# A split layer norm, an input taken by tiles, a set-up moved into the first layer and smaller attention-stage products in a two-layer transformer kernel

## What is computed

```python
def layer_norm(x, g, b):
    mu = x.mean(-1, keepdims=True)
    var = jnp.square(x - mu).mean(-1, keepdims=True)
    return (x - mu) * lax.rsqrt(var + LN_EPS) * g + b

h = layer_norm(x, emb_ln_g, emb_ln_b)
for i in range(DEPTH):                       # 2
    mix = hybrid_mixer(h, ...)               # h @ w_in, fox attention, hgrn2, @ w_out
    h = layer_norm(ALPHA * h + mix, ln1_g[i], ln1_b[i])
    ffn = peer_ffn(h, ...)                   # queries, keys, top 16, experts u and v
    ple = sigmoid(h @ ple_gate_w[i]) * (p[i] @ ple_w[i])
    h = layer_norm(ALPHA * h + ffn + ple, ln2_g[i], ln2_b[i])

# fox attention: scores q k^T * scale + c_q - c_k (c: running sum of the forget gate's log)
# hgrn2: A[t, s] = sum_k q[t,k] k[s,k] exp(b[t,k] - b[s,k]) for s <= t, with b a running sum
```

## Time and profile before

| | us |
|---|---|
| median of the runs | 3343.91 (3341.01 to 3344.86, 3 runs) |
| profiled execution | 3346.2 |
| its span, first to last instruction | 3344.4 |
| TensorE busy | 3246.8 (97%) |
| VectorE busy | 2526.8 (76%) |
| GpSimd busy | 2059.4 (62%) |
| ScalarE busy | 1388.8 (42%) |

### The profile page before, as it was taken

The page is one execution under the profiler, slowest core; times in us unless marked ns, Lnnn a source line. Parts: engine busy times, 40 slices in busy tenths (PEclk is TensorE's granted clock), DMA queues, the critical chain, the costliest instruction groups (busy, mean ns, idle before and its releaser), DMA issues. The chain is left out here.

```text
span 3344.4 us, 47104 instructions
## 1 busy us (share of the span) xinstructions
PE 3246.8 (97%) x17370; PEld 2895.4 (87%) x17370; DVE 2526.8 (76%) x4660; ACT 1388.8 (42%) x2738; POOL 2059.4 (62%) x1388
## 2 busy tenths in 40 slices
PE   5999999999999999999999999999999999999998
PEld 4787789999999988888877877899999999888886
DVE  5966359896876588888878643698769666888888
ACT  1235013466666433333312431135666664333332
POOL 5930777666677655555479136766666776555553
PEclk9999999999999999999999999999999999999999
DMA  3220224687899999999722112256888999999995
GB/s 124 88 70 14 101 76 156 229 297 293 303 330 352 350 388 375 362 370 365 279 77 88 45 39 94 83 195 225 306 299 301 337 350 357 389 372 364 370 365 195
DMA packets 312724, 817.12 MB, mean 244 GB/s; under 512 B 22320, under 2 KB 119600, under 8 KB 309168
## 3 DMA queue, kind: packets, MB, share of 16 engines
q1 hardware_dynamic: 112304, 349.02, 30.2%
q0 software_dynamic: 73728, 268.47, 20.7%
q10 hardware_dynamic: 126464, 196.63, 16.8%
HBM read 712.84 MB, written 101.19 MB: 243 GB/s over the span
## 5 line engine op out<-in xcount | busy, mean ns | idle before, releaser
L1283 POOL TENSOR_TENSOR u_lo<-panel,u_hi 128x1024 fp32r<-128x1024 f32 x256 | 618.4, 2416 | 316.3 <-ACT u_hi L1085 316.0
L595 PE MATMUL ps<-hT_hi,u_lo 128*128 128x384 f32 x2048 | 701.3, 342 | 0.0
L595 PE MATMUL ps<-hT_lo,u_hi 128*128 128x384 f32 x2048 | 685.6, 335 | 0.0
L595 PE MATMUL ps<-hT_hi,u_hi 128*128 128x384 f32 x2048 | 685.5, 335 | 0.0
L595 PE MATMUL ps<-v_hi,w_lo 128*128 128x512 f32 x1536 | 598.6, 390 | 3.1 <-DVE w_lo L1849 2.9
L595 PE MATMUL ps<-v_lo,w_hi 128*128 128x512 f32 x1536 | 598.3, 390 | 0.0
L595 PE MATMUL ps<-v_hi,w_hi 128*128 128x512 f32 x1536 | 598.3, 390 | 0.0
L1300 POOL TENSOR_TENSOR v_lo<-panel,v_hi 128x1024 fp32r<-128x1024 f32 x128 | 312.3, 2440 | 374.7 <-ACT v_hi L1147 374.6
L1147 ACT CAST v_hi<-panel 128x1024 fp32r<-128x1024 f32 x256 | 269.3, 1053 | 640.1 <-PE ps L595 634.4
L1233 POOL TENSOR_TENSOR ring_hi<-panel,cst 128x512 fp32r<-128x512 f32 x244 | 276.5, 1133 | 414.1 <-PE ps L575 257.0
L1085 ACT CAST u_hi<-panel 128x1024 fp32r<-128x1024 f32 x256 | 268.1, 1048 | 442.7 <-PE ps L595 442.6
(11 more groups left out here) (272 smaller groups left out, 5691.3 us busy)
## 6 DMA issues: line engine op xcount, KB each, us to landing
panel<-in_u SPq DMA_DIRECT2D x256, 512.0 KB, 4.3
panel<-in_v SPq DMA_DIRECT2D x256, 512.0 KB, 7.2
gate_scratch<-arena ACTq DMA_DIRECT2D x24, 2048.0 KB, 9.5
act_scratch<-arena ACTq DMA_DIRECT2D x124, 384.0 KB, 4.1
arena<-act_scratch ACTq DMA_DIRECT2D x62, 768.0 KB, 7.1
arena<-gate_scratch ACTq DMA_DIRECT2D x62, 768.0 KB, 15.3
panel<-in_w_in SPq DMA_DIRECT2D x28, 1024.0 KB, 5.2
panel<-in_wq SPq DMA_DIRECT2D x16, 1024.0 KB, 5.1
```

The source lines that it names most:

```text
L595: mm = nc.tensor.matmul(o, lhs[a], rhs[b_], start=(start and n == 0), stop=(stop and n == 2))
L1283: pr.mark(nc.gpsimd.tensor_tensor(u_lo[:, j % URING].rearrange("p c n -> p (c n)"), u_tile(j), u_hi[:, j % URING].rearrange("p c n -> p (c ...
```

## The change

The norm is split between engines: VectorE centres and multiplies by the gain, ScalarE multiplies by the reciprocal root (`normed`, and the same at the start), and the bias is no longer in h when it is transposed. It is added at the transposed chunks, where it is one number per partition (new input `biases`), by the two operations that read the banks; and h itself gets it from four new VectorE adds (`biased`) later in the stage. The last norm of the kernel keeps the old form (`tile_output`). Each tile's steps now follow each other, tile after tile. GpSimd starts a layer on `rstd_ready`, the last reciprocal, in place of `h_ready`. x is loaded by four transfers, with gains and constants between them; lower-bound logits and bias row go behind the second panel. The set-up and the casts (`set_up`) run in layer 0 after the forget gate's sum, and TensorE waits for the casts only ahead of the attention stage. Level 5 becomes four blocks of 16 in the columns of level 0, with no mask of its own. The decays of a pair of heads on the first tile go over 256 columns, ahead of the scores, instead of 128 behind them.

```diff
-MASKED = 6
+MASKED = 5
...
+        biases_s = sb("biases_s", [P, 1 + 2 * DEPTH, NC])
...
-            sp.dma_start(h[:], x.rearrange("(i p) d -> p i d", p=P)).then_inc(x_in.sem, 16)
-            sp.dma_start(lb_in[:], lbl).then_inc(lb_loaded.sem, 16)
-            for k, a in enumerate((emb_g, emb_b)):
-                sp.dma_start(lng[:, k, :], a.partition_broadcast(P)).then_inc(emb_in.sem, 16)
-            sp.dma_start(cst[:], consts).then_inc(const_in.sem, 16)
+            for i in range(NT):
+                sp.dma_start(h[:, i, :], x[i * P:(i + 1) * P, :]).then_inc(x_in[i].sem, 16)
+                if i == 0:
+                    sp.dma_start(lng[:, 0, :], emb_g.partition_broadcast(P)).then_inc(emb_g_in.sem, 16)
+                if i == 1:
+                    sp.dma_start(cst[:], consts).then_inc(const_in.sem, 16)
+            sp.dma_start(biases_s[:], biases).then_inc(biases_in.sem, 16)
...
+                if layer == 0:
+                    sp.dma_start(lb_in[:], lbl).then_inc(lb_loaded.sem, 16)
+                    sp.dma_start(lng[:, 1, :], emb_b.partition_broadcast(P)).then_inc(emb_b_in.sem, 16)
...
-            pe.wait_ge(casts.sem, casts.before)
...
+                    def decays(cols, start):
+
+                        for s in (2 * j, 2 * j + 1):
+                            o, hd = fox_s_bank(s), head_tile(s)[0]
+                            rows_ = slice(FD * (hd % 2), FD * (hd % 2) + LOW_ROW + FH)
+                            nc.tensor.matmul(o[:, 0:cols], head_row[rows_, hd:hd + 1].to_broadcast([LOW_ROW + FH, P]),
+                                             negc_parts[rows_, 0:cols], start=start, stop=False)
+
+                    if i == 0:
+                        decays(2 * P, True)
...
+                                             fkT[rows_, hd // 2, c0_:c1_], start=(k == 0 and i > 0), stop=False)
+                    if i > 0:
+                        decays(n, False)
...
-                            for top_, s0, n in ((6, 0, 32), (6, 64, 32), (7, 0, 64)):
+                            for top_, s0, n in ((5, 0, 16), (5, 32, 16), (5, 64, 16), (5, 96, 16),
+                                                (6, 0, 32), (6, 64, 32), (7, 0, 64)):
...
+            for i in range(NT):
+                act.wait_ge(var_ready.sem, i + 1)
+                nc.scalar.activation(rstd[:, i:i + 1], rstd[:, i:i + 1], ACT.Sqrt).then_inc(root_ready.sem, 1)
+                act.wait_ge(rstd_ready.sem, i + 1)
+                nc.scalar.activation(h[:, i, :], h[:, i, :], ACT.Copy, scale=rstd[:, i:i + 1]).then_inc(h_ready.sem, 1)
+            act.wait_ge(biases_in.sem, 16)
...
+                        if n == 1:
+                            ins = nc.scalar.copy(hT_hi[:, c, :], bank(g0 + c))
+                        else:
+                            ins = nc.scalar.activation(hT_hi[:, c, :], bank(g0 + c), ACT.Identity,
+                                                       bias=biases_s[:, 2 * layer + n // 2, c:c + 1])
+                        pr.mark(ins, hT_hi_ready)
+
+                def normed(i, n):
+
+                    root(n, rstd[:, i:i + 1])
+                    act.wait_ge(rstd_ready.sem, layer * rstd_ready.per_layer + rstd_ready.before + n - 2)
+                    pr.mark(nc.scalar.activation(h[:, i, :], h[:, i, :], ACT.Copy, scale=rstd[:, i:i + 1]), h_ready)
 
...
+                if layer == 0:
+                    act.wait_ge(lb_shift.sem, 1)
+                    nc.scalar.activation(lb_in[:], lb_in[:], ACT.Exp).then_inc(lb_exp.sem, 1)
...
-                    root(3 + i, rstd[:, i:i + 1])
+                    normed(i, 3 + i)
...
+                act.wait_ge(h_biased.sem, layer * h_biased.per_layer + NT + 1)
...
-                pool.wait_ge(h_ready.sem, layer * h_ready.per_layer + h_ready.before)
+                pool.wait_ge(rstd_ready.sem, layer * rstd_ready.per_layer + rstd_ready.before)
...
+            def centred(i, src, gains):
+
+                return nc.vector.scalar_tensor_tensor(out=h[:, i, :], in0=src, scalar=mv[:, i, 0:1], in1=gains,
+                                                      op0=ALU.subtract, op1=ALU.mult)
+
+            for i in range(NT):
+                dve.wait_ge(x_in[i].sem, 16)
+                for half in range(2):
+                    last = nc.vector.bn_stats(stat[:, i, 6 * half:6 * half + 6], h[:, i, half * 512:(half + 1) * 512])
+                first(last)
+                first(nc.vector.bn_aggr(mv[:, i, :], stat[:, i, :]))
+                nc.vector.tensor_scalar(rstd[:, i:i + 1], mv[:, i, 1:2], LN_EPS, None, ALU.add).then_inc(var_ready.sem, 1)
+                dve.wait_ge(emb_g_in.sem, 16)
+                first(centred(i, h[:, i, :], lng[:, 0, :]))
+                dve.wait_ge(root_ready.sem, i + 1)
+                nc.vector.reciprocal(rstd[:, i:i + 1], rstd[:, i:i + 1]).then_inc(rstd_ready.sem, 1)
             assert before[0] == dve_step.before, before[0]
...
+            dve.wait_ge(biases_in.sem, 16)
...
+                last.then_inc(lb_shift.sem, 1)
+                dve.wait_ge(const_in.sem, 16)
+                ordered(nc.vector.memset(negc_parts[:].bitcast(F32), 0.0))
+                ordered(nc.vector.memset(head_row[:].bitcast(F32), 0.0))
+                nc.vector.tensor_copy(ident_b, ident).then_inc(casts.sem, 1)
+                for r in (LOW_ROW, FD, FD + LOW_ROW):
+                    nc.vector.tensor_copy(head_row[r:r + FH, :], ident[0:FH, 0:FH])
+                nc.vector.tensor_copy(head_row[0:FH, :], ident[0:FH, 0:FH]).then_inc(casts.sem, 1)
+                nc.vector.tensor_copy(cmask_b, cmask).then_inc(casts.sem, 1)
+                dve.wait_ge(lb_exp.sem, 1)
...
+                        lo, hi_ = hT_lo[:, c, :], hT_hi[:, c, :].bitcast(F32)
+                        if n == 1:
+                            ins = nc.vector.tensor_tensor(lo, bank(g0 + c), hi_, ALU.subtract)
+                        else:
+                            ins = nc.vector.scalar_tensor_tensor(out=lo, in0=bank(g0 + c),
+                                                                 scalar=biases_s[:, 2 * layer + n // 2, c:c + 1],
+                                                                 in1=hi_, op0=ALU.add, op1=ALU.subtract)
+                        pr.mark(ins, hT_lo_ready)
+
+                def biased(i, n):
+
+                    dve.wait_ge(turned.sem, layer * turned.per_layer + n * NC + NC)
+                    pr.mark(nc.vector.tensor_tensor(h[:, i, :], h[:, i, :], lng[:, 1, :], ALU.add), h_biased)
+
                 turn(G_T1, 0)
...
+                if layer == 0:
+                    set_up()
+                    dve.wait_ge(emb_b_in.sem, 16)
+                lb_now = lb_all[:, bass.ds(layer, 1), :].rearrange("p a h -> p (a h)")
+                nc.vector.tensor_scalar(lb[:, 0, :], lb_now, LB_FLOOR, None, ALU.max)
+                step(nc.vector.tensor_scalar(lb[:, 1, :], lb_now, -1.0, 1.0, ALU.mult, ALU.add))
+                biased(0, 0)
+                biased(1, 0)
...
+                biased(2, 0)
+                biased(3, 0)
...
-                        for g in range(2):
+                        for g in range(2 if 3 + k < MASKED else 1):
...
+                    if g < 4:
+                        dve.wait_ge(h_biased.sem, layer * h_biased.per_layer + g + 1)
...
+                def tile_centred(i, roots, src=None):
+
+                    ins = centred(i, h[:, i, :] if src is None else src, lng[:, 0, :])
...
+                    pr.need(root_ready, roots)
+                    return pr.mark(nc.vector.reciprocal(rstd[:, i:i + 1], rstd[:, i:i + 1]), rstd_ready)
+
+                def tile_output(i, roots, src=None):
+
+                    pr.need(rstd_ready, tile_centred(i, roots, src))
...
-                tile_variance(0)
-                tile_scaled(0, 3)
-                tile_variance(1)
-                tile_variance(2)
-                tile_scaled(1, 4)
-                tile_variance(3)
-                tile_scaled(2, 5)
-                tile_scaled(3, 6)
-                dve.wait_ge(h_ready.sem, layer * h_ready.per_layer + h_ready.before + NT)
+                for i in range(NT):
+                    tile_variance(i)
+                    tile_centred(i, 3 + i)
 
                 turn(G_T3, 2)
+                biased(0, 2)
+                biased(1, 2)
...
+                biased(2, 2)
+                biased(3, 2)
...
-                tile_scaled(0, 7, acc0)
-                summed_variance(1)
-                tile_scaled(1, 8)
-                summed_variance(2)
-                summed_variance(3)
-                tile_scaled(2, 9)
-                tile_scaled(3, 10)
-                dve.wait_ge(h_ready.sem, layer * h_ready.per_layer + h_ready.before + 2 * NT)
+                tile_last = tile_centred if layer < DEPTH - 1 else tile_output
+                tile_last(0, 7, acc0)
+                for i in range(1, NT):
+                    summed_variance(i)
+                    tile_last(i, 7 + i)
...
```

(40 more changed lines are left out.)

98 lines of the change are left out of this document (42 added, 56 removed).

## The result

The changed kernel takes 3306.4 us (median of 4 runs, 3303.77 to 3307.4) against 3344.39 beside it: a ratio of 0.9888, 95% interval 0.9876 to 0.9901.

The account below looks back on a forecast made before the run. TensorE, 97% busy, bounds the kernel; GpSimd sets layer 0's projections up to chunk 34. Terms 20.7 - 3.9 + 4.1 + 2.3 + 2.8 - 1.5 + 0.4 - 4.0 + 2.6 = 23.5 us: 3320.5 us, range 3309 to 3332.

Parts of the forecast that it names:

- Start, 20.7: Kernel start: with x by tiles and the norm split, TensorE's first projection matmul comes at 21.1, 20.7 us earlier.
- Bias adds and set-up in the projections, 3.9 and 1.5 lost: Projection stages: VectorE's adds and set-up delay GpSimd's splits, losing 3.9 us in layer 0; adds lose 1.5 in layer 1.
- The wait of 4.9: Layer 0's projections before the change: chunk 34 ready at 139.22, due 134.3, so TensorE waited 4.9 us for GpSimd.
- Rival (b): Layer 0's projections: set-up spills, each tiny operation waiting for a whole split; stall of 6.8 us, 3327; chance 10%.
- the lock: Skill's rule: VectorE and GpSimd share a port pair, locked for a whole instruction; speaks against set-up beside GpSimd.
- Norms, 4.1, 2.3, 2.8 and 0.4: Gains in us: first norm of layer 0, first of layer 1, second of layer 0, and root waits at the end.
- Level five, +3.5: Attention stage: eight records of 16 columns at 0.045 us each add 0.11 per tile, 32 tiles, 3.5 us slower.
- The lower bound that I had named, -2: Level five in the attention stage: records of 16 at half the price, by their columns, give -2 us.
- Decays, +1.3: Attention stage: decays over 256 columns take 0.47 against 0.31 for a pair, 8 pairs, 1.3 us slower.
- Clock, 2.6 with bounds 0 and 7.8: After norms' gaps: TensorE loses 2.6 us at half clock at three places; one counted as saved, bounds 0 and 7.8.
- The range: Whole kernel: 3309 to 3332 us; low end (a) with two more clock stretches, high end (c), or (b) without clock gain.
- rival (a): Projection stages keep all gains, the adds' delays falling into GpSimd's waits: 5.4 us more, 3315; chance 12%.

Follow-up runs that it names:

- The second filler kernel: Kernel before, with shorter matmuls nobody reads in TensorE's gaps at three norms, sized to end before the transposes' input comes: 3335.7 us, ratio 0.9978.

## Why the prediction came out as it did

- **Start, 20.7:** right, 21.0 to the first matmul. What failed is the remark that a slow first stretch costs nothing, since GpSimd binds there: it cost 0.6 in one profile and 1.9 in the next. Tiles at 4.3, 8.1, 11.1 and 14.2, the last reciprocal at 17.25, ScalarE's scaling 1.15, the matmul 2.3 behind it. GpSimd's first chunk ended 1.0 ahead of it.
- **Bias adds and set-up in the projections, 3.9 and 1.5 lost:** the sums, 3.8 and 1.6, are right, and so is the mechanism, but that the sums fit so closely is luck. In layer 0 the set-up's 0.6 was not there, and 0.6 of clock at the start was, which I had at nothing. The adds alone measured 2.9 and 2.8, where I had 3.3 and, behind GpSimd's lead and its full ring, 1.5; layer 1's sum came out at 1.6 because 1.3 of the clock's gain behind the norm lies in that stage. With the clock's loss taken off, it grew from 162.9 to 165.9: the lead and the full ring took nothing off. TensorE's waits for ring_lo rose by 2.5, not 4 to 5. The wait of 4.9 that I worked out for chunk 34 is 3.8 in the trace of before, in four pieces.
- **Rival (b), and the lock:** VectorE's casts of 8x8 took 0.82 each beside GpSimd against 0.17 alone, close to the 0.77 that I used for all 21; the waits for gate products that (b) needed are not in TensorE's list.
- **Norms, 4.1, 2.3, 2.8 and 0.4:** the first and third right (4.4, 3.4). In layer 1's first norm I took transposes at half clock as the bound and got 2.3; it was 4.6. The second filler kernel shows the step that failed: with transposes at full clock the matmul comes no sooner, as GpSimd's first chunk, bound to the last tile, decides. The bound was VectorE's chain, as in layer 0.
- **Level five, +3.5:** the step that failed, by far the largest. I priced a block record by the nearest row of the trace, 0.045 us for 32 columns, and counted eight of them. They measured 0.05 together; in the nearest row 0.13 of the 0.18 us lie between the last record of 32 columns and the first of 64. Level five gives 5 us (stages less their clock loss: 112.5 and 111.6 against 114.8 and 114.3 with the level whole, 5.0 for both layers). The lower bound that I had named, -2, was too high as well: it halved the price of a record but left a price in it.
- **Decays, +1.3:** about 0.4. I had taken the difference of two pairs' durations, where their starts count.
- **Clock, 2.6 with bounds 0 and 7.8:** near the upper bound. I kept the three slow stretches because the gaps shrink only by 2 to 4 us and their transposes stay. That was enough: 2.75 in layer 0, 2.9 in layer 1 and 1.3 at the layer's boundary, 7.0. The query stream of layer 1 shortened by 4.3; 1.2 of that is a wait for ScalarE (L1135) in the first profile of before. How much of the 7.0 one execution shows is partly chance, as the losses at equal norms above say.
- **The range:** its low end adds the clock's upper end and rival (a), 3320.5 - 5.2 - 5.4 = 3309.9, and leaves level five at +3.5. With the end of -2 that I had named for it, the low end would have been 3304.4, below the 3306.4 measured, if by too small a step. With the measured values in place (level five from 2.7, its 3.5 less the copy's waits of 0.8, to -5.0: 7.7 better; decays 0.9; the streams' 7.0 less 2.6; layer 1's first norm 2.3) the forecast's sum is 23.5 + 7.7 + 0.9 + 4.4 + 2.3 = 38.8; the times say 38.0.

## What to carry to other kernels

Price a small matmul by taking a group with it and one without from the trace, not by dividing a neighbour's time by its count; if no such pair exists, let the low bound be no cost at all, for it decides the sign of an edit that swaps large products for small ones. A norm on the path can be paid twice: in its own length, and in the transposes and matmuls at its end, which lost 11.5 to 15 us at half clock with the three long norms of the kernel before and 1.4 to 5 with the shorter ones. Work moved off the path belongs where its engine idles and the engine that it slows down (here GpSimd) is ahead: the same four adds cost 5.7 us in one place and nothing in another, and exponentials moved to the end of a step, where they looked idle, cost 33.

## What was not expected of the hardware

- Eight fp32 records of 16 columns beside six of 32 and 64: 0.05 us more for the group (0.49 against 0.44), while the group repeated costs 0.50.
- The granted clock behind one and the same wait of 2.3 us: 1.0 in one layer and 0.50 in the other, within one execution, and otherwise in the next.
- VectorE's casts of 8x8 took 0.17 alone and 0.82 beside GpSimd's splits, which stayed at 1.29. An add of 128x1024 took 2.1 there instead of 1.22, and the two GpSimd operations beside a pair of them 2.16 and 2.02 instead of 1.29 and 1.04. Which of the two pays is not always the same: in the query stage of the changed kernel (363.7) a pair of these adds took 1.22 each, and the split beside them 3.40.
- A fall of the clock with 1.7 us of loss cost only 0.2 where TensorE follows GpSimd, while 0.6 to 1.9 us of half pace at the start of the same stage cost their full length.
